# Hybrid and MoE block: router logits from rows before the norm, expert rows fetched pair by pair and turned by VectorE, an 18th weight place

## The reference, cut to what matters

```python
h = layer_norm(DEEPNORM_ALPHA * h + mix, ln1_g[l], ln1_b[l])
ffn = hier_moe(h, w_grp[l], b_grp[l], w_rtr[l], b_rtr[l], w1[l], w3[l], w2[l])
h = layer_norm(DEEPNORM_ALPHA * h + ffn, ln2_g[l], ln2_b[l])

def hier_moe(h, w_grp, b_grp, w_rtr, b_rtr, w1, w3, w2):
    grp_prob = softmax(t @ w_grp + b_grp)            # 4 groups, the best one is taken
    g_prob, g_sel = top_k(grp_prob, 1)
    exp_logits = (t @ w_rtr + b_rtr)                 # 4 x 8 experts, the best two of the group
    e_prob, e_sel = top_k(softmax(in_grp), 2)
    gate = g_prob * e_prob / sum(e_prob)
    hid = silu(t @ w1[e]) * (t @ w3[e])              # 1024 -> 256 for each of 32 experts
    y = sum_e (hid * combine[e]) @ w2[e]             # 256 -> 1024
```

## Time and profile before

| what | value |
|---|---|
| span of the profiled execution | 1303.9 us |
| PE busy | 1269.3 us, 97% |
| DVE busy | 559.9 us, 43% |
| ACT busy | 486.9 us, 37% |
| POOL busy | 115.5 us, 9% |
| DMA | 307.40 MB, mean 236 GB/s |
| expert stage of layer 0, layer 1 | about 581 to 807 us, 1070 to 1293 us |

### The profile page before, as it was taken

One profiled execution on the slowest core, in us unless ns is written; L12 is line 12 of the kernel. 1 busy time (PEld: TensorE's weight loads), 2 busy tenths in 40 slices (PEclk: granted clock), 3 DMA queues, 4 the chain that ended last, 5 costly groups with the idle time before them and its releaser, 6 DMA issues.

```text
span 1303.9 us, 19404 instructions
## 1 busy us (share of the span) xinstructions
PE 1269.3 (97%) x7567; PEld 815.6 (63%) x7567; DVE 559.9 (43%) x1226; ACT 486.9 (37%) x1066; POOL 115.5 (9%) x167
## 2 busy tenths in 40 slices
PE   9999999999999999999999998999999999999996
PEld 7888588885787877454344443788877554444432
DVE  3335223262676584342232215678485342222224
ACT  3346343462753245212223323663235312223232
POOL 0000000000014321000000000004322000000000
PEclk9999999999999999979999999999999999999998
DMA  9753162332521124749999999231132859999994
GB/s 367 150 179 112 50 268 97 130 111 78 205 98 67 66 98 172 308 170 377 420 420 420 422 416 407 100 113 67 66 130 99 341 213 397 419 421 420 422 420 195
DMA packets 48848, 307.40 MB, mean 236 GB/s; under 512 B 5897, under 2 KB 6409, under 8 KB 16752
## 3 DMA queue, kind: packets, MB, share of 16 engines
q1 hardware_dynamic: 43760, 288.61, 56.0%
q0 software_dynamic: 3200, 8.16, 2.8%
q10 hardware_dynamic: 1792, 9.31, 1.9%
HBM read 301.05 MB, written 8.59 MB: 237 GB/s over the span
## 4 chain that ended last, share of the span: by engine, by line
PE 80%; DVE 13%; ACT 5%; issue 2%; DMA 1%; ACTq 0%; DVEq 0%; SPq 0%
PE ps L1150 22%; PE ps L1840 18%; PE ps L1867 9%; PE ps L1417 4%; PE ps L1190 4%; PE ps L1909 2%; PE ps L1930 2%; PE ps L1118 2%; DVE projT L2792 1%; DVE small L2791 1%; PE ps L1158 1%; PE ps L1649 1%; PE ps L1849 1%; DVE projT L2783 1%; PE ps L1540 1%
## 5 line engine op out<-in xcount | busy, mean ns | idle before, releaser
L1150 PE MATMUL ps<-hT,ring 128*128 128x272 f32 (+1 forms) x1760 | 416.8, 390 | 0.6 <-ACT hT L2027 0.6
L1150 PEld LDWEIGHTS ps<-hT,ring 128*128 128x128 f32 x1760 | 327.1, 190 | 62.6 <-issue 7.0
L1840 PE MATMUL ps<-ring,arena 128*64 128x512 f32 x416 | 139.4, 600 | 0.0
L3157 DVE TENSOR_TENSOR xo<-ps,xo 128x512 fp32r<-128x512 f32 x64 | 42.9, 689 | 99.3 <-ACT xo L2465 99.3
L3278 POOL TENSOR_TENSOR arena<-projT,cst 32x272 f32<-32x272 f32 x104 | 71.6, 689 | 114.1 <-DVE projT L2770 101.0
L1840 PE MATMUL ps<-projT,arena 128*64 128x512 f32 x240 | 80.0, 597 | 0.0
L3148 DVE TENSOR_TENSOR arena<-arena,ps 128x256 f32<-128x256 f32 x32 | 13.5, 422 | 140.0 <-ACT arena L2452 139.4
L1840 PEld LDWEIGHTS ps<-ring,arena 128*64 128x64 f32 x416 | 40.1, 137 | 52.0 <-issue 51.2
L2450 ACT ACTIVATE arena<-ps 128x256 f32<-128x256 f32 x32 | 12.3, 386 | 138.7 <-PE ps L1840 138.7
L1417 PE MATMUL ps<-ring,projT 128*128 128x512 f32 x128 | 56.6, 596 | 0.0
L1190 PE MATMUL ps<-ring,arena 128*128 128x512 f32 x128 | 55.9, 593 | 0.0
(11 more groups left out here) (518 smaller groups left out, 2045.8 us busy)
## 6 DMA issues: line engine op xcount, KB each, us to landing
ring<-experts SPq DMA_DIRECT2D x72, 1024.0 KB, 16.2
ring<-w_in SPq DMA_DIRECT2D x62, 1024.0 KB, 5.4
projT<-experts SPq DMA_DIRECT2D x48, 1024.0 KB, 15.6
arena<-experts SPq DMA_DIRECT2D x22, 1024.0 KB, 12.8
prm<-experts SPq DMA_DIRECT2D x22, 1024.0 KB, 15.9
ring<-w_out SPq DMA_DIRECT2D x16, 1024.0 KB, 4.8
spare<-experts SPq DMA_DIRECT2D x12, 1024.0 KB, 14.5
lent<-experts SPq DMA_DIRECT2D x8, 1024.0 KB, 10.1
```

The source lines that it names most:

```text
L1150: mm = pe.matmul(ps[:, chunk_bank(blk, l, j), 0:ncols], w[:, j % 2, k, :], hT[:, k, T - ncols:T], start=(k == 0), stop=(k == KC - 1))
L1840: mm = pe.matmul(ps[64 * e:64 * e + 64, 0, :], xg[:, 4 * h + k, i % 2, 64 * e:64 * e + 64], w[e][:, k // 2, 512 * (k % 2):512 * (k % 2) + ...
L3157: v.tensor_tensor(low, ps[:, 4 + half, :], high, ALU.subtract).then_inc(s("pair_rows_copied"), 1)
```

## The change

The edit has five parts:

1. The router's weights are multiplied with the norm's gain (`fold`); the logits come from rows before the norm, and mean, root and bias enter by `adjusted`, with column sums made by PE (`router_sums_made`).
2. The turns and logits of tiles 1 and 0 move into the projection; group and expert choice are made for the early tiles first and then for tile 2 alone. `norm_scaled` of tile 2 comes behind its group choice. Filler matmuls are sized anew.
3. Pairs 4 to 15 get their rows by one indirect DMA a pair (`slot_tokens` into `pair_rows`, two buffers) and DVE turns them in blocks of 32 x 32 into `xg` (`turn_tokens`); `gather_two` is left for pairs 2 and 3 alone.
4. The next group is prepared at the second pair of a group instead of the third, with `psel` in two buffers.
5. An 18th weight place lies in `hT`; load 14 waits for the norm alone, load 17 for the logits and the first fetched rows. `xselT` leaves `lent`, whose place is then used to the end.

```diff
-ALL_SLOTS = 17
-LAST_USE = {LENT: 57, ONCE[1]: 75, CONSTS_ROOM: 79, NORMS_ROOM: 79}
+ALL_SLOTS = 18
+LAST_USE = {ONCE[1]: 75, TURNED_ROOM: 75, CONSTS_ROOM: 79, NORMS_ROOM: 79}
+SLOT_FACTS = 2 * PER_GROUP + 1
...
+        def turned_pairs():
+            return range(PAIRS_A_GROUP, PAIRS)
+        def fetched_by(l, i=None):
+            return 16 * ((PAIRS - PAIRS_A_GROUP + 1) * l + (1 if i is None else i - PAIRS_A_GROUP + 2))
+        def places_left(i):
+            return i - PAIRS_A_GROUP + 4
... SP
                     if j == 7 + MORE_SLOTS + ITEMS_WO:
                         sp.wait_ge(layer_normed, normed_at[l, 1, 2, 1])
-                        sp.wait_ge(rows_fetched, 16 * (GROUPS * l + 1))
+                    if j == 7 + MORE_SLOTS + ITEMS_WO + 3:
+                        sp.wait_ge(s("logits_done"), 2)
+                        sp.wait_ge(rows_fetched, fetched_by(l))
... PE
+                        if t == 2:
+                            pe.wait_ge(s("router_vec_ready"), 2 + half)
+                        else:
+                            pe.wait_ge(mean_ready, mean_at[l, 1, t])
+                def router_sums_made():
+                    pe.wait_ge(s("router_vec_ready"), 1)
+                    pe.matmul(ps[:, 1, 192:264], ones, router_sums.rearrange("p a n -> p (a n)"), start=True, stop=True)
...
+                    if t == (0 if l < LAYERS - 1 else 2):
+                        router_turn(0, 1)
...
+                            if t == 2 and i == ITEMS_WO - 1 and c == 0:
+                                pe.wait_ge(s("groups_chosen"), 1)
+                                count_groups(tiles_of(l)[:-1])
-                        if t == 2 and i == 1:
-                            router_turn(0, 1)
-                        if t == 2 and i == 2:
+                        if t == 2 and i == 0:
+                            if l < LAYERS - 1:
+                                router_turn(1, 0)
+                            router_sums_made()
                             router_logits(0, 1)
+                        if t == 2 and i == 1 and l < LAYERS - 1:
+                            router_logits(1, 0)
...
-                for p, t in list(enumerate(norm_order(l)))[1:]:
-                    if t == 2:
-                        keep_busy(5, *([384, 384] if l < LAYERS - 1 else 4 * [448]))
-                    router_turn(p, t)
-                    router_logits(p, t)
-                keep_busy(5, 384, 384)
-                pe.wait_ge(s("groups_chosen"), 1)
+                pe.wait_ge(s("experts_chosen"), 1)
+                count_experts(tiles[:-1])
+                last = len(tiles) - 1
+                router_turn(last, 2)
+                router_logits(last, 2)
+                keep_busy(5, 448, 384)
+                pe.wait_ge(s("groups_chosen"), 2)
+                count_groups([2])
+                keep_busy(5, 512, 384)
...
-                keep_busy(5, 448)
                 first_tokens()
-                keep_busy(5, 512, 512, 512)
+                keep_busy(5, 512, 512)
+                pe.wait_ge(s("experts_chosen"), 2)
+                count_experts([2])
+                keep_busy(5, 256)
-                if l == LAYERS - 1:
-                    keep_busy(5, 448, 448)
...
                 turn_group(0)
-                keep_busy(4, *([256] if l < LAYERS - 1 else [384, 512, 512, 384]))
+                keep_busy(4, 448)
...
+                    if i < PAIRS_A_GROUP:
+                        pe.wait_ge(s("pair_tokens_copied"), copies_of(i) - (h == 0))
+                    else:
+                        pe.wait_ge(s("row_places"), places_left(i))
...
-                        if i % 2 and i + 1 < PAIRS:
-                            gather_two(i + 1, 0)
+                        if i == 1:
+                            gather_two(2, 0)
... DVE
+                fold()
+                for p, t in enumerate(norm_order(l)[:-1]):
+                    norm_sums(t, 1, lambda half: (s("out_projected"), p + 1 + half))
+                    scaled(p, t)
+                V(v.memset(xrows, 0.0))
+                v.wait_ge(s("logits_done"), 1)
+                V(v.tensor_copy(router_sums[:, 0, :], ps[:, 1, 192:228]))
+                V(v.tensor_tensor(router_sums[:, 1, :], ps[:, 1, 228:264], prm2("br"), ALU.add))
+                for t in tiles[:-1]:
+                    adjusted(t)
+                group_choice(early)
+                expert_choice(early, early_slots)
+                norm_means(2, 1, lambda half: (s("out_projected"), nt + half), lambda ins: V(ins, s("router_vec_ready")))
+                mixer_ends(v)
+                v.wait_ge(s("router_in_turned"), 2 * last + 2)
+                V(v.tensor_copy(h2T[:, 4:8, COL[2]:T], ps[:, 7, :].rearrange("p (k n) -> p k n", k=4)), s("router_vec_ready"))
+                norm_centered(2, 1)
+                v.wait_ge(s("logits_done"), 2)
+                adjusted(2)
+                group_choice(final)
+                norm_scaled(2, 1)
+                slots_in(final)
+                select(0, [2])
+                expert_choice(final, first_group_tokens)
...
+                def turn_tokens(i):
+                    v.wait_ge(rows_fetched, fetched_by(l, i))
+                    v.wait_ge(up_used, 2 * PAIRS * l + 2 * (i - 2) + 2)
+                    rows = pair_rows[i % 2].rearrange("p (k j r) -> p k j r", j=4, r=32)
+                    for j in range(4):
+                        for slots in range(4):
+                            here = slice(32 * slots, 32 * slots + 32)
+                            ins = v.transpose(xg[32 * j:32 * j + 32, :, i % 2, here], rows[here, :, j, :])
+                    ins.then_inc(s("row_places"), 1)
...
                         if i:
                             rows_out(i - 1)
+                        if i + 2 in turned_pairs():
+                            turn_tokens(i + 2)
... POOL
+                for i in turned_pairs():
+                    group, q = i // PAIRS_A_GROUP, i % PAIRS_A_GROUP
+                    g.wait_ge(s("pair_gates_copied"), group + 1)
+                    g.wait_ge(s("row_places"), max(3, places_left(i - 2)))
+                    g.wait_ge(rows_fetched, fetched_by(l, i - 1 if i > PAIRS_A_GROUP else None))
+                    g.indirect_dma_start(pair_rows[i % 2], None, normed_rows,
+                                         bass.IndirectOffsetOnAxis(ap=slot_tokens[:, group % 2, q:q + 1], axis=0),
                                          bounds_check=T - 1, oob_is_err=False).then_inc(rows_fetched, 16)
+                    if q == 1 and group > 1:
+                        send(l, group - 2)
```

More of the change, by code:

```diff
@@ L1385, in mix_chunk, with count_experts @@
+                def count_experts(some):
+                    for t in some:
+                        for u in range(tiles_of(l)[0], t + 1):
+                            m = ROWS[u]
+                            mm = pe.matmul(ps[:, 0, 32 * t:32 * t + 32], counting[0:m, 0 if u == t else 1, :],
+                                           marks[0:m, u, :], start=(u == tiles_of(l)[0]), stop=(u == t))
+                    mm.then_inc(s("places_counted"), 1)
                 def mix_chunk(c):
@@ L1810, in experts_all @@
                     drain()
+                    for q, t in enumerate(norm_order(l)):
+                        for half in range(2):
+                            if q:
+                                pe.wait_ge(s("router_in_copied"), 2 * len(tiles) - 2 + 2 * q + half)
+                            turn_rows(t, half)
+                    pe.wait_ge(s("router_in_copied"), 4 * len(tiles) - 1)
                     pe.wait_ge(s("all_lined"), 1)
@@ L3000, in select, with c, each, size @@
-                def select(g):
-                    for t in tiles:
+                early, final = slice(t0, 2), slice(2, 3)
+                def c(i, w, ts=slice(t0, 3)):
+                    return lg[:, ts, i:i + w]
+                def each(i, w, ts=slice(t0, 3)):
+                    return bc(lg[:, ts, i], w, 2)
+                def size(ts):
+                    return ts.stop - ts.start
+                def fold():
+                    wr = prm2("wr").rearrange("p (k n) -> p k n", k=KC)
+                    biased = arena[:, 0:KC * 36].rearrange("p (k n) -> p k n", k=KC)
+                    V(v.tensor_tensor(biased, wr, bc(prm2("ln1_bc"), 36, 2), ALU.mult))
+                    V(v.tensor_tensor(wr, wr, bc(prm2("ln1_gc"), 36, 2), ALU.mult))
+                    V(v.tensor_reduce(router_sums[:, 0, :], wr.rearrange("p k n -> p n k"), AX, ALU.add))
+                    V(v.tensor_reduce(router_sums[:, 1, :], biased.rearrange("p k n -> p n k"), AX, ALU.add),
+                      s("router_vec_ready"))
@@ new lines, in expert_choice @@
+                def expert_choice(ts, between=None):
+                    V(v.tensor_scalar(c(56, 4, ts), whole(group_marks)[:, ts, :], -NEG, NEG, ALU.mult, ALU.add))
+                    V(v.tensor_tensor(c(64, 32, ts).rearrange("p t (a b) -> p t a b", a=4),
```

(9 more changed lines are left out.)

315 lines of the change are left out of this document (166 added, 149 removed).

## The result

The changed kernel takes 1323.58 us (median of 4 runs, 1322.1 to 1324.8) against 1306.23 us for the kernel before (the three runs above and one more): a ratio of 1.0125, 95% interval 1.0107 to 1.0143. It is 17 us slower. A second set of 4 runs gave 1321.33 us against 1307.24, ratio 1.0107 (1.0081 to 1.0132). The profiled execution has a span of 1322.5 us, 18.6 over the 1303.9 of before; that of the second set 1318.8, 14.9 over.

A forecast was written before the change was run, and what follows sets the result against it. The full weight stream bounds the stage, so its restart and the bytes behind it decide time. Restarts 0.5 us later and 3.5 earlier give 3.0, the end 1.2: 4.2 us off the median 1304.44, 1300.3; range 1291 to 1310.

The forecast's parts named there:

- step 4: Store and fetch of tile 2: store 3.5 us, fetch 5.5 and 4.9; rows land at 1068.7 (layer 1) and 576.8 (layer 0).
- step 6: Bytes behind the restart: one load fewer offsets extra fetched rows; restart to last landing stays 212.5 and 210.3 within 1 us.
- step 5: Gather and first half at full clock, 5.7 us from data to restart; bound 2.9 us a layer for the lower clock.
- step 8: End of the stage: down(15) starts at once on the last landing, gaining 0.7 us in layer 1, 0.5 in layer 0.
- Steps 1 to 3: Last projection to pair selection: VectorE late, chain shorter; gains about 1 us in layer 1 and 2.5 in layer 0.
- rival (b): Released loads hold up store and fetch, idle TensorE gathers at half clock: half the delay likelier, 1309 us; chance 0.22.
- proof against it: Fetch landing beyond 1071 or 579, granted clock falling at the gather in both layers, or 1090:1270 below 415 GB/s.
- The two terms that I weighed: Behind the restart: 18th place saves one load, 2.5 us; extra rows of groups 1 to 3 cost 2.0 to 2.4 us.
- The bound of 2 us for the software queue's mean rate: Behind the restart: small transfers at the software queue's mean, 224 GB/s, would cost 2 us more a layer.
- Step 7: Inside the stage: VectorE turns of 0.4 us, 6.4 a pair, are covered; gathers leaving TensorE only add waits for weights.
- (c): In the stage, lighter TensorE gives places back sooner and speeds the stream: 8 us beyond the forecast, 1292; chance 0.06.
- (d): In the stage, VectorE turns cost 0.9 us or more each, exceeding the pair's 15 us: 1375 us; chance 0.02.

The follow-up runs named there:

- e10: Kernel before with parts 3, 4 and 5 of the edit alone, router chain as before: 1313.07 us, ratio 1.0047.
- e2: Changed kernel, but loads 14 to 16 wait until the store of tile 2 has landed: 1319.43 us, ratio 1.0087.
- e5: Changed kernel with 17 weight places instead of 18, the new one in hT unused: 1327.22 us, ratio 1.0152.
- e1: Changed kernel, but loads 14 to 16 wait for the first fetched rows, as before the change: 1309.85 us, ratio 1.0022.
- e11: Kernel before with parts 1 and 2 and the 18th place, released with loads 14 to 16 behind the first fetched rows: 1302.15 us, ratio 0.9959.
- e7: Changed kernel with one of the sixteen 32x256 turns of each pair 4 to 15: 1320.75 us, against 1321.33 unedited.
- e14: e11 once more, unedited: 1301.62 us, ratio 0.9969.
- e13: e11 with two more filler matmuls, 256 columns ahead of the early expert count and 128 behind it: 1301.50 us, ratio 0.9959.
- e3: Changed kernel with eight more filler matmuls of 512 columns before the first gather: 1318.30 us, ratio 1.0084.
- e6: Changed kernel with token numbers of pairs 4 to 15 meaning no row, so their fetches move nothing: 1311.71 us, ratio 1.0032.

## Why the prediction was wrong

It said 1300.3 us, 1291 to 1310; the time was 1323.6. Two steps failed, step 4 and step 6; step 5 fell with the first, and the 1.2 us of step 8 were no gain.

- **Steps 1 to 3, the chain, held.** Less the common shift (11.1 us in layer 1, 1.7 in layer 0; layer 1 first here), the second add ends at 1053.0 (I said 1053.2) and 561.8 (561.9), the groups are chosen at 1057.2 (1057.2) and 566.0 (565.9), the tokens are ready at 1061.1 (1060.85) and 569.9 (569.6), the pair selection at 1066.3 (1065.9) and 575.1 (574.8). The stall for the mean is 1.68 us (I said 1.6).
- **Step 4, "3.5, nearer to idle, because both start together".** This is the term that failed. The store took 7.3 and 6.6 us; three loads of 2.49 are 7.5. I had the two rows, 2.6 and 5.0, took the 5.0 as the upper end, and asked what the store meets but not how much was queued: nothing in the trace of before showed a store beside three fresh loads. In e10, issued behind the third load, it went up to 9.8. The fetch came out at 4.8 and 5.2 for 4.9 and 5.5, beside loads of which about four tenths were left (I had said about half); but that was in part luck. I had it start 4.3 us behind the release, and it started 8.3 and 7.6 us behind, because the store was late. In layer 0 of e2 it started 3.7 us behind the first load and took 7.8, near the 8.4 end. The rows landed 3.9 us (layer 0) and 2.9 us (layer 1) later than I said.
- **Step 5.** I took the full clock. TensorE waited 6.2 and 5.6 us, and the clock was at 0.50 in both layers: data to restart 8.3 and 7.4 us for 5.7, by which the half clock costs 2.6 and 1.7, where my bound was 2.9. I had tied the clock to the filler and the tile of 16 rows; it hung on how long the fetch would be late. Steps 4 and 5 are one event, and rival (b) had it with its mechanism, at 0.22. What the prediction named as proof against it came true: the fetch beyond 1071 and 579 (1071.5 and 580.6 less the shift), the clock down in both layers. The restarts are 8.1 us late in sum (first profile), between the 12 us of (b) at its full size and the 6 us, half of it, that I took as the end of the range.
- **Step 6, "Restart to last landing stays 212.5 and 210.3 within 1 us".** From restart to down(14) it is 2.8 and 2.3 us longer. By the prediction's own measure, the last landing, it is about 215.1 and 212.3 us for 212.5 and 210.3, so 2.6 and 2.0. The two terms that I weighed were right: the place is worth 2.3 a layer (e5), and the rows of the pairs are 0.9 MB a layer over before (software queue 9.95 MB for 8.16), 2.1 us. What I put at nothing is the first 30 us, in which the DMAs are 0.8 and 1.2 MB short, 1.9 and 2.9 us. There the stream goes as fast as TensorE gives places back, and two things hold it up. In layer 1 loads 14 to 17 have all landed at the late restart, where before some were under way (0.66 MB in the first 20 us). In layer 0 they had landed in the kernel before too, as I wrote, so this is no part of it there. In both layers the preparation of the next group, moved into the second pair by part 4, makes TensorE give back the next places up to 2.2 and 1.4 us later (0.82 and 0.57 MB in the ten us from 20 to 30). The prediction has no term for part 4 at all. The other runs agree: in e1 and e11 loads are under way at the restart and the first 20 us have 415 to 424 GB/s, but the ten us behind them have 382 and 387 in e1, with part 4, and 425 and 421 in e11, without. No run has part 4 alone (e10 has it together with part 3), so its share is read from the traces, not tested. In layer 0 some 1 us more stays unexplained. The bound of 2 us for the software queue's mean rate was the right size by another cause.
- **Step 7 held.** The turn is 0.435 us, 7.0 a pair (I said 0.4 and 6.4), wholly covered (e7); the gathers that left TensorE gave nothing but waits (12 us idle in 160). The estimate of 0.27 us for a turn beside my 0.4 was too low. Rivals (c) and (d) fell by this; but (c) had a point for the first 30 us, where places given back late do slow the stream, only that TensorE was later there and not sooner. The sum of (d) should also read 1377 and not 1375.
- **Step 8, the end, was wrong, by 1.2 us.** down(15) starts 5.8 us behind down(14), 1297.58 to 1303.40, in both kernels 5.8 (1279.09 to 1284.90): between them lie ScalarE's and VectorE's passes over the rows of down(14) and their sum on TensorE, not the last load.

Of the slowdown of 13 to 15 us, then, 8.0 are steps 4 and 5 against the restart of before (I had -3.0), and 5.1 to 6.8 are step 6 (I had 0). The rest of the first profile's 18.6 is chance. The median of 1323.6 lies beyond the range because the end of the range had 6 us for the restarts, nothing for step 6 and 1.2 us of gain from step 8.

## What to carry to other kernels

Before loads are released earlier, list the small transfers that the next step waits for, and price each at the whole backlog that is queued with it, not at the one row nearest to idle: half a megabyte took 6.6 and 7.3 us when issued among three loads of 1 MB, 8.4 and 9.8 us behind the third, and alone 2.6. Two edits that alone give -1.1 and +5.9 us can cost some 10 us more together, where the one makes a transfer late and the other sends the traffic into which it then falls. A weight stream whose places are all full before its consumer starts gains nothing from having been still earlier. And once the consumer runs, small work that is moved ahead of the release of a place holds the stream up, even where the consumer has idle time later: here 1 to 2 us a layer as the traces have it.

## What the runs showed of the hardware

- The same instructions, started within 0.02 us of the same time, went on at a granted clock of 1.00 or 0.50 from one execution to the next (e1 and the second profile of the changed kernel, from 563 us in layer 0). TensorE had waited 0.44 us for the early expert marks shortly before in both. The fall lasts 9 us or more, and marks to restart is 5.0 us longer with it (30.8 for 25.8, e14 and e13), through fillers that stand on the path.
- A fetch of up to 128 rows takes 3.4 to 4.5 us with idle DMA engines, 4.5 to 5.4 beside loads that are half drained (the changed kernel, e3 and e5), and 7.8 to 8.1 beside fresh ones (e2). A pair fetch that moves no row still takes 7.4 us beside the full stream (median; 8.1 with rows, e6 and the changed kernel): most of its time is not its bytes.
